# Gated output projections of two layers: eight quarter products replaced by seven, with the gate applied to the separate sum

## What is computed

```python
mod_l = jnp.split((sc @ mod_w[i] + mod_b[i])[:, None, :], N_MOD, axis=-1)
...
x = x + mod_l[2] * m_l                       # m_l = mixed @ ev_w_out or od_w_out
ctx = ctx + mod_c[2] * m_c                   # even layer only
...
modulate(x, norm_ffn[i], mod_l[3], mod_l[4]) # rows for router and experts
```

## Time and profile before

| what | us |
|---|---|
| three runs | 2024.54, 3323.06, 2023.17 (median 2024.54) |
| profiled execution | 2022.98 |
| its span in the trace | 2021.2 |
| TensorE busy | 1893.0 (94%) |
| VectorE busy | 1188.9 (59%) |
| ScalarE busy | 642.9 (32%) |
| GpSimd busy | 249.4 (12%) |
| stretch of the even projection after the meeting | 1207.65 to about 1284 |
| stretch of the odd projection after the meeting | 1756.70 to about 1804 |

### The profile page before, as it was taken

How to read it: one execution, slowest core, us unless ns; L and a number is a source line. 1 busy time by engine, 2 the same in 40 slices (tenths; PEclk the granted TensorE clock), 3 DMA queues, 4 the chain that set the end, 5 groups by cost and what they waited for, 6 DMA issues and landing times.

```text
span 2021.2 us, 28938 instructions
## 1 busy us (share of the span) xinstructions
PE 1893.0 (94%) x10950; PEld 1038.0 (51%) x10950; DVE 1188.9 (59%) x1908; ACT 642.9 (32%) x1274; POOL 249.4 (12%) x260
## 2 busy tenths in 40 slices
PE   7999999999999999899998999899997999999993
PEld 4554875544444444455645764533334678645330
DVE  2001777487787653358754643677756657456774
ACT  2011762200000001242313641266643556323551
POOL 3000110011111000012200002511102000041101
PEclk9999999999999999999999999999998989999997
DMA  8632100677766442411111002689965020148995
GB/s 267 161 84 83 54 12 22 224 253 252 240 237 235 150 171 94 133 42 42 42 42 47 18 19 89 260 323 365 361 246 209 1 84 2 35 163 347 385 416 199
DMA packets 108472, 323.88 MB, mean 160 GB/s; under 512 B 9063, under 2 KB 43015, under 8 KB 89904
## 3 DMA queue, kind: packets, MB, share of 16 engines
q1 hardware_dynamic: 77920, 190.56, 26.3%
q0 software_dynamic: 25168, 112.53, 15.6%
q10 hardware_dynamic: 5248, 18.94, 2.4%
HBM read 291.48 MB, written 35.76 MB: 162 GB/s over the span
## 4 chain that ended last, share of the span: by engine, by line
PE 72%; DVE 7%; issue 7%; DMA 6%; PEld 4%; PEldq 2%; ACT 1%; POOL 1%; POOLq 0%; DVEq 0%; SPq 0%; ACTq 0%
PE ps L3435 15%; PE ps L466 7%; PE ps L2056 6%; PE ps L2866 6%; PE ps L1186 5%; PE ps L1232 4%; PE ps L3236 4%; PE ps L1207 4%; PE ps L364 3%; DMA X<-moe_rows,row_token 3%; PE ps L2887 3%; PE ps L335 2%; PE ps L2032 2%; PEld ps L1779 2%; PE ps L1779 1%
## 5 line engine op out<-in xcount | busy, mean ns | idle before, releaser
L3435 PE MATMUL ps<-wide 128*128 128x512 f32 (+1 forms) x736 | 306.5, 575 | 1.9 <-issue 1.7
L3435 PEld LDWEIGHTS ps<-wide 128*128 128x128 f32 x736 | 138.3, 190 | 166.3 <-issue 164.1
L2866 PE MATMUL ps<-wide,X 128*32 x448 | 197.5, 594 | 2.1 <-DVE X L3037 2.1
L2866 PE MATMUL ps<-Z,X 128*32 128x512 f32 x1344 | 197.9, 594 | 0.0
L2056 PE MATMUL ps<-wide 128*128 128x512 f32 (+1 forms) x384 | 149.1, 545 | 0.5 <-issue 0.5
L1540 DVE SCALAR_TENSOR_TENSOR Z<-Z,wide 128x2048 f32<-128x2048 f32 x56 | 131.6, 2350 | 2.8
L1186 PE MATMUL ps<-T 64*128 64x256 f32 (+1 forms) x888 | 110.0, 378 | 8.7 <-DVE nm L1325 6.8
L1779 PE MATMUL ps<-wide 128*128 128x512 f32 x256 | 113.8, 602 | 2.1 <-issue 1.1
L744 ACT ACTIVATE T<-ps 128x512 f32<-128x512 f32 (+2 forms) x139 | 70.7, 536 | 131.0 <-PE ps L1779 111.5
L1257 ACT ACTIVATE T<-T,nm 128x768 f32<-128x768 f32 (+3 forms) x112 | 86.7, 775 | 77.6 <-DVE nm L1325 77.6
L2866 PEld LDWEIGHTS ps<-wide,X 128*32 128x32 f32 x448 | 47.0, 110 | 124.1 <-issue 124.1
(11 more groups left out here) (421 smaller groups left out, 3353.8 us busy)
## 6 DMA issues: line engine op xcount, KB each, us to landing
wide<-in_experts SPq DMA_DIRECT2D x64, 1024.0 KB, 10.7
Z<-in_mod_w POOLq DMA_DIRECT2D x32, 1024.0 KB, 5.3
T<-in_experts SPq DMA_DIRECT2D x32, 1024.0 KB, 11.1
X<-in_mod_w POOLq DMA_DIRECT2D x16, 1024.0 KB, 5.4
moe_out<-X ACTq DMA_DIRECT2D x28, 512.0 KB
wide<-in_w_down SPq DMA_DIRECT2D x12, 1024.0 KB, 6.8
wide<-in_w_gate SPq DMA_DIRECT2D x22, 512.0 KB, 5.9
wide<-in_w_up SPq DMA_DIRECT2D x22, 512.0 KB, 6.9
```

The costliest lines, as they stand in the source:

```text
L2866: last = pe.matmul(ps[rows, t % 2, :], mo.xT[:, c, rows], w_rows, start=(c == 0), stop=(c == DK - 1))
L3435: last = pe.matmul(self.gu.bank(u)[:, columns], w, self.rhs(c)[:, columns], start=(c == 0), stop=(c == DK - 1))
```

## The change

Both stages become `GatedBySeven`. With n the number of tile pairs (3 in the even layer, 2 in the odd), even tiles and odd tiles of the rows are the two row halves; the matrix is cut into four quarters b11, b12, b21, b22 of 512x512. TensorE computes seven products of a row half sum and a quarter sum, each n parts of four matmuls, where the `Linear` had eight. VectorE makes the sums: S1 to S4 over the rows (128 x 512n) and T1 to T4 over the quarters (128 x 2048). ScalarE copies P1 four times side by side as the start of the separate results; VectorE adds P2, P3, P6 and P5, multiplies the results by the gate, adds them to `k.X`, and then gates and adds P7 and P4 to the odd tile by way of a buffer `product`. The ring gets two loads, two slots passed over for T2 and T1, and two loads: six places instead of four. The raising of the gains moves from the start of VectorE's stage to behind T3. `begin` runs all n parts of P1 whatever number it is given.

```diff
+class GatedBySeven(Stage):
+    SUMS = "S1", "S2", "S4", "T1", "T2", "S3", "T3", "T4"
...
+        self.PARTS = [(p, i) for p in ("P1", "P2", "P3", "P6", "P5") for i in range(n)] + [(p, i) for i in range(n) for p in ("P7", "P4")]
...
+        first = 0 if n == 2 else 4
+        late = [(4 - first) + (v + (2 if n == 3 else 0)) % 4 for v in range(2 * n)]
+        self.banks = [u % 8 for u in range(5 * n)] + late
...
+        self.b11, self.b22 = quarter(0, 0), quarter(1, 1)
+        self.t2 = k.rg.pass_over(2)
+        self.t1 = self.t2 + 1
+        self.b12, self.b21 = quarter(0, 1), quarter(1, 0)
...
+        self.norm = TileNorm(k, norm, self.tile_done, first, inside=True)
...
+    def tile_done(self, eng, t):
+        if t % 2:
+            self.after_add(eng, "P4", t // 2, "total")
+        else:
+            self.after_add(eng, "total", t // 2, 0)
...
+    def begin(self, pe, tiles):
+
+        self.k.rg.await_landed(pe, self.b11)
+        for i in range(self.n):
+            self.part(pe, "P1", i, self.rows(0, 0), self.b11)
+
+    def tensor(self, pe):
...
+        for i in range(n):
+            self.part(pe, "P5", i, self.s1, self.t1)
+        self.after_sum(pe, "T4")
+        for i in range(n):
+            self.part(pe, "P7", i, self.s3, self.b12, 0 if i else 1)
+            self.part(pe, "P4", i, self.rows(1, 1), self.b21, 0 if i else 2)
+            if i:
+                self.norm.turn(pe, i - 1)
+        pe.drain().then_inc(k.weights_used, 2)
+        self.between(pe, self.norm)
+        self.norm.tensor(pe)
...
+    def vector(self, dve, ch):
...
+        made(self.s1, self.rows(0, 1), self.rows(1, 1), ALU.add)
...
+        made(self.s2, self.s1, self.rows(0, 0))
...
+        made(self.s4, self.rows(1, 0), self.s2)
...
+        made(t1, b12, b11)
...
+        made(t2, b22, t1)
+        for i in range(n):
+            self.after_part(dve, "P2", i)
+            self.after_copy(dve, i)
+            add(("P2", i), self.result(2 * i)[:, 0:512], self.bank("P2", i))
+        made(self.s3, self.rows(0, 0), self.rows(0, 1))
+        made(b12, b22, b12)
+        self.row_stores.raise_gains(dve)
...
+            add(("P3", i), self.result(2 * i)[:, 512:D], self.bank("P3", i))
...
+        made(b21, b21, t2)
+        for i in range(n):
+            self.after_part(dve, "P6", i)
+            add(("P6", i, 0), self.result(2 * i)[:, 512:D], self.bank("P6", i))
+            add(("P6", i, 1), halves(self.result(2 * i + 1)), twice("P6", i))
+        for i in range(n):
+            self.after_part(dve, "P5", i)
+            add(("P5", i, 0), self.result(2 * i)[:, 512:D], self.bank("P5", i))
+            add(("P5", i, 1), self.result(2 * i + 1)[:, 512:D], self.bank("P5", i))
+        if self.gates_landed:
+            self.gates_landed(dve)
+        for i in range(n):
+            gate = self.gates[:, 0 if 2 * i < ST else 1, :]
+            for row in (0, 1):
+                t = 2 * i + row
+                add(("gated", i, row), self.result(t), gate, ALU.mult)
+                add(("total", i, row), k.X[:, t, :], self.result(t))
+        for i in range(n):
...
+            multiply(("P7", i, "gated"), halves(self.product), twice("P7", i), halves(gate))
+            add(("P7", i, "total"), x, self.product)
+            if i:
+                self.norm.tile(dve, ch, 2 * i - 1)
+            self.after_part(dve, "P4", i)
+            multiply(("P4", i, "gated"), self.product[:, 0:512], self.bank("P4", i), gate[:, 0:512])
+            add(("P4", i, "total"), x[:, 0:512], self.product[:, 0:512])
+            self.norm.tile(dve, ch, 2 * i)
+            if i:
+                self.norm.take(dve, "dve", i - 1)
+        self.norm.tile(dve, ch, 2 * n - 1)
+        self.norm.vector(dve, ch)
+
+    def scalar(self, act, ch):
+        for i in range(self.n):
+            self.after_part(act, "P1", i)
...
+            act.activation(both, self.bank("P1", i).unsqueeze(1).to_broadcast((P, 4, 512)), ACT.Copy).then_inc(self.k.firsts_copied.sem, 1)
         self.norm.scalar(act, ch)
...
-        even.then = Linear(k, hT, DK, A["ev_w_out_2"][0], D, allt, gated_take(k.gatebc), ["dve"] * 12,
-                           norm=mod_sets(0, 1, True))
...
+        even.then = GatedBySeven(k, A["ev_w_out_2"][0], allt, mod_sets(0, 1, True), k.gatebc, gate_rows.landed)
...
-        odd.then = Linear(k, hT, DK, A["od_w_out_2"][0], D, seq, gated_take(oddgate), ["dve"] * 8, norm=mod_sets(1, 1, False))
+        odd.then = GatedBySeven(k, A["od_w_out_2"][0], seq, mod_sets(1, 1, False), oddgate)
```

More of the change, by code:

```diff
@@ L2390, in gpsimd, with landed @@
             pool.dma_start(dst, src).then_inc(self.k.gate_rows.sem, 16)
-    def vector(self, dve, ch):
-        dve.wait_ge(self.k.gate_rows.sem, self.base + 16 * len(self.pairs))
+    def landed(self, eng):
+        eng.wait_ge(self.k.gate_rows.sem, self.base + 16 * len(self.pairs))
 class RowStores(Stage):
@@ L2436, in gpsimd, with raise_gains @@
             pool.dma_start(self.rows_out[t * P:(t + 1) * P, :], row).then_inc(k.rows_stored.sem, 16)
-    def vector(self, dve, ch):
+    def raise_gains(self, dve):
         k = self.k
@@ L3664, in two_blocks @@
         k.sums_made, k.partials_added, k.parts_full = tally("sums_made"), tally("partials_added"), tally("product_parts_full")
+        k.firsts_copied = tally("first_products_copied")
         k.mods_ready = sem("mods_ready")
@@ L3816, in two_blocks @@
         add(Together(k, start, shrink))
[L3818 to L3827, removed]
         def gate_loads(l, m, n, to=None):
@@ L3881, in two_blocks @@
         add(Together(k, Load(k, [(k.X[:, :, :], away)]), even))
-        even.then = Linear(k, hT, DK, A["ev_w_out_2"][0], D, allt, gated_take(k.gatebc), ["dve"] * 12,
-                           norm=mod_sets(0, 1, True))
-        head = [Loading(k, gate_loads(0, 2, 2)), row_stores(0, even.then, 2), even.then]
+        gate_rows = Loading(k, gate_loads(0, 2, 2))
+        even.then = GatedBySeven(k, A["ev_w_out_2"][0], allt, mod_sets(0, 1, True), k.gatebc, gate_rows.landed)
+        head = [gate_rows, row_stores(0, even.then, 2), even.then]
         oddgate = k.Z[:, 9920:9920 + D].unsqueeze(1)
```

90 lines of the change are left out of this document (added).

## The result

The changed kernel took 2050.72 us (median of four runs, 2048.89 to 2055.07) against 2024.19 for the kernel before: 1.0128 of it, with a 95% interval of 1.0111 to 1.0145. So it is 26 us slower, where 2047, with a range from 2030 to 2060, had been forecast; that is clear of the noise and less than the 2% that the forecast gave 0.96. One of the four runs of the kernel before took 3323.06, the other three 2023.17 to 2024.54, so the median hardly feels it.

The account below looks back on a forecast made before the run. TensorE's matmuls bound the old kernel; VectorE's late tail and GpSimd's row operations were to bound the new one. Losses of 15.1 (even) and 7.7 (odd), sum 22.8, on 2024.5 gave 2047.3, said as 2047, range 2030 to 2060.

Parts of the forecast that it names:

- What bounds it: TensorE in both projections: idle nowhere before, it would stand idle some 15 and 10 us before the first turn.
- The matmuls: TensorE loses 12 of 96 matmuls (even) and 8 of 64 (odd): 10.3 and 6.9 us, together 17.2.
- The run of twelve and eight steps: VectorE's gated and total steps queued ahead of P7 and P4: 15.1 us in the even layer, 10.1 in the odd.
- The tail of the norm: VectorE's last tiles, taking turns with GpSimd's row operations: last turns 14.1 us late (even) and 5.1 (odd).
- The router: VectorE's router steps wait for GpSimd's row operations to end; line 2563 comes 15.1 us late (even), 7.7 (odd).
- rival 1: VectorE's short two-input steps are not blocked by GpSimd: loss 15 us, hence 2040; chance 0.13.
- The ring's order: Odd input projection: slot 0's load is issued before the one awaiting gathered rows; taken as 0, bound 4.65 us.
- Rival 4: Worse: clock low through the router's idling, stores delay the gathers: 10 us, with 5 for the clock, 2062; chance 0.11.
- rival 3: The matmuls' gain comes through, VectorE's last tile following TensorE: 2024.5 - 17.2 = 2007; chance 0.08.
- The sign: Even layer: the loss would turn to a gain with gated and total steps below 15.1 - 10.3 us.
- Rival 2: VectorE's order alone sets the last turns, GpSimd and VectorE hardly disturbing each other: 5.0 + 1.2, hence 2031; chance 0.11.

Follow-up runs that it names:

- the odd layer alone: Seven products in the odd layer only, the even layer keeping its Linear, against the kernel before: ratio 1.0040, 8.1 us slower.
- TensorE kept busy: The changed kernel with added identity matmuls (64 even, 42 odd) in TensorE's idle stretch ahead of the first turn: 1.0136 of the kernel before.
- the kernel before with plain rows: The kernel before without GpSimd's two operations (gain and shift) on each normed row, stores kept: 0.9986 of the kernel before.
- the kernel with plain rows: The changed kernel without GpSimd's two operations (gain and shift) on each normed row, stores kept: 1.0028 of the kernel before, 2030.98 us.
- without the run: The changed kernel without the twelve (odd layer: eight) VectorE steps gating P1, P2, P3, P6, P5 results and adding them to X: 1.0059 of the kernel before.
- gated once: The changed kernel with TensorE and VectorE ordered by pair, P7 and P4 added to the odd tile before gating: 1.0055 of the kernel before.

## Why the prediction came out right, step by step

**What bounds it.** Right. TensorE had no idle time before and has 15.24 and 10.13 us now ahead of its first turns, against forecasts of 15 and 10. The chain that ended last runs through VectorE and calls the stretched steps partly VectorE and partly "issue":

```profile
1277.00 3.39 DVE X L874
...
1280.53 2.53 issue
...
1283.77 3.15 DVE X L874
```

The 2.53 of "issue" are line 1068's 2.64.

**The matmuls.** Right: the projection begins with 16 records instead of 24 in the odd layer, and its meeting comes 7.39 us behind the start instead of 10.80, 3.4 nearer.

**The run of twelve and eight steps.** Right in length (from 1255.78 to 1270.87, 15.1) and in what follows it: GpSimd's first operation starts at 1271.85 net, forecast 1271.5, and its last one ends at 1310.5 net, forecast 1311.8. In the odd layer the first starts at 1798.6 net, forecast 1798.35.

**The tail of the norm.** This term was mis-sized: forecast 14.1 and 5.1 us on the last turn, measured 17.1 and 9.4. I had followed the taking of turns tile by tile but let P4's totals go at 0.70, without a reason. Behind pair 0 they took 3.15 and 3.17 in the even layer and 3.15 in the odd one, though each stands just ahead of GpSimd's operation in the rows, and the last scaling 1.88 and 1.89 instead of 0.75. Tile 1 was where the forecast had it (1278.0 net, forecast 1277.95), tile 2 already 2.3 late (1284.6 against 1282.3).

**The router.** Wrong in its mechanism. It was to be held until GpSimd's end and to add 1.0 and 2.6 us. With the norm's tail later, GpSimd was nearly through when the router's short steps came: line 2742 waited once (1.34 in the even layer, 2.15 in the odd one), as line 2537 had before (2.30), and line 2769 comes 16.4 and 9.4 us late, where 15.1 and 7.7 were forecast. So apart from that one wait no hole of 2 us appeared among the short steps, and whether a short step with two SBUF inputs waits, which parts the forecast from rival 1, no run shows: none met a GpSimd operation.

**The ring's order.** Taken at 0, and no cost shows. It turns the order ahead of the odd input projection, which lies between the last turn of the even layer and the start of the odd projection: 458.9 us here, 457.0 before, 457.4 with the odd layer alone (the old order) and 456.0 with TensorE kept busy (the new order). The 4.65 us taken as its bound belong to the experts' gather, which is as before (4.76).

**Forgotten.** Behind the gather the even layer loses another 2.5 us until the odd projection (16.4 at the router, 24.0 - 5.1 = 18.9 there). TensorE's first records of the experts took 1.07 where the kernel before had 0.61 to 0.63 for the same form; the granted clock was 0.54 from 1339 to 1345, and 1.00 from 1317 to 1322 before. Rival 4 had named a low clock behind the router's idle time. That the change brings it is not shown: the kernel before with plain rows has 1.07 there as well, the changed one with TensorE kept busy 0.63. The odd layer gives 1.3 back behind its router, 8.1 in all at the end; why stays open. Sum 18.9 + 8.1 = 27.0 and the 5.1 make the 32.1 between the spans of 2053.3 and 2021.2; on the medians the loss is 26.5 against a forecast of 22.8.

**Luck in the sum.** Two terms were wrong against each other. The last turns came 3.0 and 4.3 us later than forecast, and the router, which was to add 1.0 and 2.6, added nothing (-0.7 and 0.0). So at the router the error is only 1.3 and 1.7.

**Slips in the working.** In rival 1, 5.1 - 2.2 is 2.9 and not 3.4, so its time is 2039.3. A row's 6.3 on GpSimd is two operations and the 1.43 between rows, which already holds the 0.54 of issue.

**The rivals.** The matmuls' gain (rival 3) came in part, and only for a kernel that had neither the gate's steps nor GpSimd's: 17.2 us forecast, 14.4 below the kernel before and 12 below the kernel before with plain rows. The sign was to turn in the even layer with less than 4.8 us of gate steps; with none of them, but GpSimd at work, that stretch is still 5.7 us longer than before. Rival 2, only the queue, is the kernel with plain rows. Its 2031 and the 2030.98 measured agree by luck: the last turns were to be 5.0 and 1.2 us late and were 6.6 late and 0.4 early, and the kernel before took 2025.86 beside it. In the changed kernel the engines do disturb each other. Rival 1, short steps not blocked, stays undecided.

## What to carry to other kernels

Ahead of moving sums to VectorE, look for GpSimd in the same stretch: while GpSimd runs an operation that reads two, a VectorE step that reads two operands in SBUF (and here the scaling by `tensor_scalar` as well) costs the rest of that operation on top of its own length (about 2 us each here; GpSimd's operations cost 18 to 26 us in all), so price such steps by the neighbour's instruction. Starting GpSimd earlier by moving VectorE's steps in among its operations brought nothing (1.0148); taking steps away did (1.0059 without the run, 1.0055 gated once). A gain on the engine that bounds the kernel is worth what the next engine in the queue can follow.

## What the runs showed of the hardware

How strictly the engines take turns was not expected. Where GpSimd has two operations in a row and VectorE has SBUF steps queued, each waits for the end of the other's instruction: 3.39, 2.64, 3.15 and 2.65 instead of 1.22, 0.75, 0.69 and 0.75, with GpSimd's second operation at 2.68 to 3.21 instead of 2.35. Its first operation was not lengthened in the changed kernel (2.35 to 2.38), not even where VectorE's add stands 0.24 us ahead of it. The same two GpSimd operations on six and four rows cost 3 us where TensorE was last and 18 to 26 us where VectorE was. And of TensorE's clock: after 15 us of idling it was granted 0.50, the lower level, and sixteen transposes took 3.68 instead of 1.97; keeping it at 1.00 there gained no time.
